# A recurrent mixer in chunks of 64 tokens, with each chunk as an affine map of the state

## What is computed

```python
def wkv7_scan(r, w, k, v, a, b):
    """S_t = S_{t-1} diag(w_t) + (S_{t-1} a_t) b_t^T + v_t k_t^T ; y_t = S_t r_t.
    All inputs (B, S, H, N) f32; state (B, H, N_v, N_k)."""
    def step(state, inp):
        r_t, w_t, k_t, v_t, a_t, b_t = inp
        sa = jnp.einsum('bhvk,bhk->bhv', state, a_t)
        state = (state * w_t[:, :, None, :] + sa[..., None] * b_t[:, :, None, :]
                 + v_t[..., None] * k_t[:, :, None, :])
        return state, jnp.einsum('bhvk,bhk->bhv', state, r_t)
    s0 = jnp.zeros((B, H, N, N), jnp.float32)
    _, ys = lax.scan(step, s0, xs)
    return jnp.moveaxis(ys, 0, 1)
```

## Time and profile before

| | us |
|---|---|
| median of 3 runs | 3302.31 (3301.39 to 3302.34) |
| the profiled execution | 3304.38 |
| its span, first to last instruction | 3302.4 |
| TensorE, matmul | 3173.8 (96%) |
| VectorE | 1703.5 (52%) |
| ScalarE | 1066.7 (32%) |
| GpSimd | 1972.7 (60%) |

### The profile page before, as it was taken

The page is one execution under the profiler, slowest core; times in us unless marked ns, Lnnn a source line. Parts: engine busy times, 40 slices in busy tenths (PEclk is TensorE's granted clock), DMA queues, the critical chain, the costliest instruction groups (busy, mean ns, idle before and its releaser), DMA issues.

```text
span 3302.4 us, 54354 instructions
## 1 busy us (share of the span) xinstructions
PE 3173.8 (96%) x19314; PEld 2521.1 (76%) x19314; DVE 1703.5 (52%) x2741; ACT 1066.7 (32%) x1988; POOL 1972.7 (60%) x2607
## 2 busy tenths in 40 slices
PE   6998999999999999899999999999999999999999
PEld 4766777777888888577778888887667777888887
DVE  4456777765554335542645554446551635565345
ACT  2153434432221113542635321113552535331112
POOL 4624333336588885246465888886327373898886
PEclk8999999999999999999999999999999999999999
DMA  5341111112233232112121322232102121223322
GB/s 210 138 163 51 46 40 40 40 34 77 93 98 100 95 96 65 32 52 83 40 82 58 96 96 96 95 96 83 45 27 95 46 83 46 93 93 100 98 95 96
DMA packets 70794, 265.22 MB, mean 80 GB/s; under 512 B 7744, under 2 KB 7872, under 8 KB 67520
## 3 DMA queue, kind: packets, MB, share of 16 engines
q1 hardware_dynamic: 68288, 257.59, 23.7%
q10 hardware_dynamic: 2304, 4.83, 0.4%
HBM read 260.29 MB, written 2.10 MB: 79 GB/s over the span
## 4 chain that ended last, share of the span: by engine, by line
PE 83%; DVE 9%; ACT 5%; issue 1%; DMA 1%; SPq 0%; DVEq 0%; ACTq 0%
PE psum_a L579 10%; PE psum_a L583 10%; PE psum_a L582 10%; PE psum_d L579 7%; PE psum_d L583 6%; PE psum_d L582 6%; PE psum_d L645 5%; PE psum_a L737 3%; PE psum_d L840 2%; PE psum_a L767 2%; PE psum_a L771 2%; PE psum_a L770 2%; PE psum_a L608 1%; PE psum_a L611 1%; PE psum_a L612 1%
## 5 line engine op out<-in xcount | busy, mean ns | idle before, releaser
L3383 POOL TENSOR_TENSOR w_lo<-raw,w_hi 128x256 fp32r<-128x256 f32 x1736 | 1425.7, 852 | 36.3
L3377 POOL TENSOR_TENSOR mark<-mark 128x1 f32<-128x1 f32 x432 | 105.2, 244 | 1248.0 <-PE psum_a L579 627.7
L579 PE MATMUL psum_a<-h_hi,w_hi 128*128 128x512 f32 x1600 | 631.9, 395 | 0.0
L583 PE MATMUL psum_a<-h_hi,w_lo 128*128 128x512 f32 x1600 | 623.7, 390 | 0.0
L582 PE MATMUL psum_a<-h_lo,w_hi 128*128 128x512 f32 x1600 | 623.3, 390 | 0.0
L3378 POOL TENSOR_SCALAR w_hi<-raw 128x1024 fp32r<-128x1024 f32 x434 | 459.6, 1059 | 33.3 <-DMA raw<-in_weights 33.3
L579 PEld LDWEIGHTS psum_a<-h_hi,w_hi 128*128 128x128 f32 x1600 | 300.8, 188 | 71.7 <-issue 10.7
L582 PEld LDWEIGHTS psum_a<-h_lo,w_hi 128*128 128x128 f32 x1600 | 300.9, 188 | 63.2 <-issue 2.2
L583 PEld LDWEIGHTS psum_a<-h_hi,w_lo 128*128 128x128 f32 x1600 | 300.7, 188 | 63.2
L579 PE MATMUL psum_d<-split,w_hi 128*128 128x512 f32 x848 | 329.9, 389 | 0.0
L582 PE MATMUL psum_d<-split,w_hi 128*128 128x512 f32 x848 | 329.9, 389 | 0.0
(11 more groups left out here) (407 smaller groups left out, 5524.7 us busy)
## 6 DMA issues: line engine op xcount, KB each, us to landing
raw<-in_weights SPq DMA_DIRECT2D x434, 512.0 KB, 3.4
plain<-in_ada SPq DMA_DIRECT2D x20, 1024.0 KB, 6.9
arena<-in_ada SPq DMA_DIRECT2D x4, 1024.0 KB, 16.9
x<-in_x SPq DMA_DIRECT2D x1, 2048.0 KB, 12.2
x<-in_x ACTq DMA_DIRECT2D x1, 2048.0 KB, 9.9
out<-x SPq DMA_DIRECT2D x8, 256.0 KB, 3.5
arena<-in_pe ACTq DMA_DIRECT2D x2, 512.0 KB, 3.6
const<-in_const ACTq DMA_DIRECT2D x1, 906.0 KB, 8.5
```

Source lines behind the costliest of these rows:

```text
L579: m = pe.eng.matmul(dst, wh, hi(t), start=t == 0, stop=False)
L583: m = pe.eng.matmul(dst, wl, hi(t), start=False, stop=t == k - 1)
L3377: eng.tensor_tensor(b.mark[:, 1:2], b.mark[:, 0:1], b.mark[:, 0:1], ALU.add)
L3383: m = eng.tensor_tensor(lo[:, part], b.raw[:, s, part], hi[:, part].bitcast(F32), ALU.subtract)
```

## The change

The chunks become 64 tokens long (eight instead of four), and a chunk is brought into the form of an affine map of the state, so that the chain is one product for each chunk:

- In the levels the four chunks with their `first`, `second`, `third` go. In their place stand six `step` products (two 64x64 products each, with one VectorE operation on 64 columns each), two at each of k=1 to 3, and one batch of outputs at k=4 (`outputs`, fourteen products, added by `dve_rwkv_outputs`).
- The maps themselves are made for all chunks at once: `inputs` between `g2` and gate of the next round, `maps` between gate and branch, with `act_rwkv_inputs`, `act_rwkv_outputs` on ScalarE and `dve_rwkv_transitions` (six operations) on VectorE.
- The start of the inverse takes 64x64 products on both sides (`pe_units`), as the inverse needs no block beyond 64. The two corners, the diagonal and the four map chunks go; two sets of `pe_units`, the turned AR (`pe_own_rows`), four transposes and the values product come.
- One scan over 512 columns, with zeros at the chunk starts in a tile `R_ONES`, replaces four scans and two column operations; two exponentials over 512 columns replace eight over 128 and two small ones. Three memsets set this up ahead of round 0.
- In the tail the order becomes gate, `inputs`, gate, `maps`, two gates in quarters with the six steps between the quarters, `outputs`, half a gate, mean, half a gate, variance. The gates of the tail now go through ring "a".

The diff, cut to the added lines of what is spoken of here:

```diff
+def pe_units(pe, ring, *terms, width=HD):
+    tiles = [pe.tile(ring) for _ in range(2)]
+    pe.eng.wait_ge(tiles[1].free, pe.emptied(tiles[1]))
+    for v in range(4):
+        for k, (lhsT, rhs) in enumerate(terms):
+            for n, (row, out) in enumerate(((0, 0), (1, 1), (0, 1), (1, 0))):
+                m = pe.eng.matmul(tiles[row].ps[ROWS[out], v * width:(v + 1) * width], lhsT(v, row, out), rhs(v, row, out),
+                                  start=k == 0, stop=k == len(terms) - 1)
+                if k == len(terms) - 1 and v == 3 and n >= 2:
+                    m.then_inc(tiles[row].full, pe.up("full_" + ring))
+    return tiles[1]
...
+def pe_own_rows(pe, ring, lhsT, rhs, chunks):
+    tl = pe.tile(ring)
...
+    for c in chunks:
+        for r in ROWS:
+            m = pe.eng.matmul(tl.ps[r, c * HD:(c + 1) * HD], lhsT(r, c), rhs(r, c), start=True, stop=True)
+    m.then_inc(tl.full, pe.up("full_" + ring))
+    return tl
...
         pe, b = self.pe, self.b
...
+        pe, b = self.pe, self.b
+        G, H = block(b.R_GH[:, :, 0]), block(b.R_GH[:, :, 1])
+        pe.eng.wait_ge(self.solved.free, pe.taken(self.solved))
+        pe_units(pe, "d", (G, lambda v, row, out: b.R_BL[ROWS[row], 2 * v + out]), width=P)
+        self.state = pe_units(pe, "d", (block(b.R_BL[:, :, 0]), H), (block(b.R_KN), block(b.R_VN)))
+        self.local = pe_units(pe, "a", (H, block(b.R_BL[:, :, 1])), (block(b.R_VN), block(b.R_KA[:, :, 1])))
+    def states(self, c):
...
+        return self.b.R_EQ[:, 0] if c == 1 else self.b.R_S[:, c]
+    def step(self, c):
+        pe, b = self.pe, self.b
+        pe.eng.wait_ge(self.state.free, pe.taken(self.state))
+        tl = self.state = pe.tile("d")
...
+        for r in ROWS:
+            m = pe.eng.matmul(tl.ps[r, 0:HD], b.R_PR[r, c, 0], self.states(c)[r], start=True, stop=True)
+        m.then_inc(tl.full, pe.up("full_d"))
+    def outputs(self):
         pe, b = self.pe, self.b
...
+    A, R, B, K = block(AR[:, :, 0]), block(AR[:, :, 1]), block(chunks(b.R_BH)), block(chunks(b.R_KH))
     more = j + 1 < KD
     pe_features(pe, "a", "g2", of(b.s_hi, b.s_lo, 1), 1)
+    if chain:
+        chain.inputs()
     pe_features(pe, "a", "gate", H)
+    if chain:
+        chain.maps()
     pe_features(pe, "d", "branch", of(b.s_hi, b.s_lo, 2), 2)
     pe.eng.wait_ge(pe.sem["rk_ready"], pe.due("rk_ready"))
     pe_plain(pe, "d", b.pair, b.R_T)
...
         else:
             pe.eng.wait_ge(normal.free, pe.taken(normal))
...
+        z = pe_units(pe, "d", (block(b.R_LT), block(b.R_TN)))
         inverse = pe_turned(pe, [b.R_TN[:, 2 * v:2 * v + 2].rearrange("p u t -> p (u t)") for v in range(4)])
...
+        if chain and k <= 3:
+            chain.step(2 * k - 1)
+        if chain and k == 4:
+            chain.outputs()
         if k == 2 and more:
             pe_rwkv_receptance(pe)
         if k == 4 and more:
             pe_rwkv_value(pe)
         if k in (2, 4) and not more:
             pe_features(pe, "a", "gate", H)
...
+        if chain and k == 5:
+            pe_rwkv_mean(pe)
         pe.eng.wait_ge(inverse.free, pe.taken(inverse))
         pe.eng.wait_ge(z.free, pe.taken(z))
...
+        normal = pe_units(pe, "d", (block(b.R_TW), block(b.R_Z)))
+        if chain and k <= 3:
+            chain.step(2 * k)
         if k == 3 and more:
             pe_rwkv_length(pe)
...
+    for src in (b.R_V, b.R_BH, b.R_KH):
+        turned = pe_turned(pe, [src[:, q * P:(q + 1) * P] for q in range(NQ)])
+    pe_units(pe, "d", (B, R))
+    maps = pe_units(pe, "d", (K, lambda v, row, out: AR[ROWS[row], 2 * v + out]), width=P)
+    pe_own_rows(pe, "a", lambda r, c: AR[r, c, 0], lambda r, c: b.ident[r, r], range(8))
     pe.eng.wait_ge(normal.free, pe.taken(normal))
...
+    inverse = pe_turned(pe, [b.R_TN[:, 2 * v:2 * v + 2].rearrange("p u t -> p (u t)") for v in range(4)])
+    pe.eng.wait_ge(turned.free, pe.taken(turned))
+    pe.eng.wait_ge(maps.free, pe.taken(maps))
+    values = pe_units(pe, "a", (block(b.R_KA[:, :, 0]), block(b.R_VN)))
...
+    pe_features(pe, "a", "gate", H)
+    chain.inputs()
+    pe_features(pe, "a", "gate", H)
+    chain.maps()
+    for first in (1, 4):
+        tl = pe.tile("a")
...
+        for n in range(4):
+            m = pe_product(pe, tl.ps, "gate", *H, KD, None, part=range(2 * n, 2 * n + 2))
+            if n < 3:
+                chain.step(first + n)
+        m.then_inc(tl.full, pe.up("full_a"))
+    chain.outputs()
+    tl = pe.tile("a")
...
+    pe_product(pe, tl.ps, "gate", *H, KD, None, part=range(0, 4))
     pe_rwkv_mean(pe)
...
+    a.eng.wait_ge(a.sem[a.last], a.own())
+    a.eng.activation(b.R_PB[:, :, 1:], chunks(b.R_CUM), ACT.Exp, scale=-DECAY).then_inc(a.sem["act_step"], a.up("act_step"))
+    a.eng.wait_ge(a.sem[a.last], a.own())
+    a.eng.activation(b.R_CUM, b.R_CUM, ACT.Exp, scale=DECAY).then_inc(a.sem["decays"], a.up("decays"))
...
+        v.eng.tensor_tensor_scan(b.R_CUM, b.R_ONES, b.R_SW, 0.0, ALU.mult, ALU.add)\
...
     if step == 2:
...
+def dve_rwkv_maps(v):
+    b = v.b
+    both = v.each(b.const[:, C_MASK4 + 2 * P:C_MASK4 + 3 * P], 4)
+    inclusive = v.each(b.const[:, C_MASK4 + 2 * P + HD:C_MASK4 + 3 * P], 4)
+    for row in range(2):
...
+        v.eng.tensor_tensor(other_rows(b.R_BL[:, :, 1], row), v.units(HD), inclusive, ALU.mult)\
...
+    for row in range(2):
...
+        v.eng.tensor_tensor(other_rows(b.R_KA.rearrange("p u m t -> p u (m t)"), row), v.units(P), both, ALU.mult)\
...
+def dve_rwkv_transitions(v, j):
+    b, AR, eye = v.b, v.b.R_AR[j % 2], v.each(v.b.const[:, C_EYE:C_EYE + HD], 4)
+    for row in range(2):
...
+        ps = v.units(P)
...
+        v.eng.tensor_tensor(other_rows(b.R_PR[:, :, 0], row), ps[:, :, 0:HD], eye, ALU.add)\
...
+        v.eng.tensor_tensor(other_rows(b.R_PR[:, :, 1], row), ps[:, :, HD:], other_rows(AR[:, :, 1], row), ALU.add)\
...
+    ends = b.R_E[j % 2].rearrange("p (v o) -> p v o", o=2)
+    for row in range(2):
...
+        v.eng.tensor_tensor(other_rows(b.R_EQ, row), v.units(HD), ends[:, :, row].unsqueeze(2).to_broadcast([P, 4, HD]), ALU.mult)\
...
 def dve_rwkv_state(v, j, c):
     b = v.b
...
+    v.eng.scalar_tensor_tensor(b.R_S[:, c + 1], v.bank()[:, 0:HD], b.R_E[j % 2][:, c:c + 1], b.R_EQ[:, c], ALU.mult, ALU.add)\
...
+def dve_rwkv_outputs(v):
+    b = v.b
...
+    v.eng.tensor_tensor(b.R_Y[:, HD:], v.bank()[:, HD:], b.R_Y[:, HD:], ALU.add).then_inc(v.sem["free_d"], v.up("free_d"))
 def dve_rwkv(v, j):
...
+    b = v.b
     more = j + 1 < KD
     dve_rwkv_prepare(v, j)
+    if j:
+        dve_rwkv_transitions(v, j - 1)
...
+            v.eng.tensor_tensor(other_rows(b.R_Z, row), v.units(HD), level, ALU.mult).then_inc(v.sem["free_d"], v.up("free_d"))
+        if j and k <= 3:
+            dve_rwkv_state(v, j - 1, 2 * k - 1)
+        if j and k == 4:
+            dve_rwkv_outputs(v)
         if k == 1:
             dve_rwkv_receptance(v, j)
...
+            v.eng.tensor_tensor(dst, dst, v.units(HD), ALU.add).then_inc(v.sem["free_d"], v.up("free_d"))
+        if j and k <= 3:
+            dve_rwkv_state(v, j - 1, 2 * k)
         if k in (1, 3) and more:
...
+    dve_rwkv_mixed(v, KD - 2)
+    dve_rwkv_transitions(v, KD - 1)
+    for c in range(1, 7):
         dve_rwkv_state(v, KD - 1, c)
...
+        dve_rwkv_low(v, c - 1)
+    dve_rwkv_outputs(v)
     dve_rwkv_centered(v)
     dve_rwkv_low(v, KD - 2)
     dve_rwkv_normed(v, KD - 1)
```

396 lines of the change are left out of this document (112 added, 284 removed).

## The result

The changed kernel takes 3312.66 us, median of 20 runs (3302.24 to 3320.79); the kernel before takes 3303.82 in 20 runs beside them (3300.3 to 3309.75). The ratio is 1.0024, 95% interval 1.0017 to 1.0032: slower by 8.8 us, inside the range of 3286 to 3318, but not the "no change" of the forecast. The profiled execution is one of the longer ones: 3317.57 us, span 3315.8, 4.9 us above the median.

The account below looks back on a forecast made before the run. VectorE's string was taken to set the level starts, TensorE to bound only part of the stage. Before round 0 -4.5, round 0 -2.2, rounds 1-6 +13.8, round 7 -0.6, tail -6.0: +0.5 us, forecast 3302.8, range 3286 to 3318.

Parts of the forecast that it names:

- The clean sum: Round 2 at full clock, all stretches added: +4.7 + 0 - 1.6 - 2.2 + 0.9 - 1.9 = -0.1 us, no gain.
- its clock terms for the rounds: Rounds 1 to 6, per round: +2.5 us half clock behind k=5, -0.5 already paid today, +0.4 for falls between k=1 and k=2.
- head: Start of a round, g2 to the first set of k=1: `inputs` and `maps` products lie on TensorE's path, loss 4.7 us.
- The reading that round 0 shows what the levels take without a chain: Levels of round 0 before the change: VectorE sets level starts, so a whole chain costs only 4 us a round.
- the length wait: Ahead of round 0, TensorE's wait before the first length product: falls from 4.01 us to about 1.
- its signs of being wrong: Wait under 2 us or full clock at k=5, head under 20 us, or rounds more than 2 from 63 us.
- I allow 0.4 a round for falls between k=1 and k=2: Rounds 1 to 6, early levels: an allowance of 0.4 us a round for TensorE's clock falling there.
- The falls behind k=5: From k=5 to the next round: half clock behind the longer wait, 2.3 to 3 us a round, taken 2.5.
- the slower rival: The clock also falls between k=1 and k=2, 1.7 us each; 3316 us with a dearer 128-column set; chance 0.24.
- Said -2.2: Round 0: only the new ending and start count, -2.2 us.
- -4.5 ahead of round 0: Ahead of round 0: wide exponentials 2.0, one scan 1, clock 1.5 us saved; -4.5 us (-5.5 to -2).
- changes of tiling: Into and out of 64-row work on TensorE: four more changes a round, 0.3 us together (0 to 0.6).

Follow-up runs that it names:

- the two filled kernels: Changed kernel and kernel before, each with unused idle-time products put into TensorE's waits ahead of k=2 and k=5 (before: k=2 in round 0 only): 3285.28 and 3300.17 us.
- the filled kernel: Changed kernel with unused TensorE products, four ahead of the wait before k=2 and six ahead of the wait before k=5: 3285.28 us.
- the last experiment: The version with three moves, with the wide scan and two wide exponentials taken apart into four scans and eight exponentials of 128 columns: 3264.67 us.
- the version with three moves: Changed kernel with VectorE's receptance behind the sums of k=1, reciprocal's string behind the last masks, two finishing operations from k=2 to k=4: 3263.09 us.

## Why the prediction was wrong by this much

**What held.** The clean sum. Without its clock terms for the rounds (6 x 2.4 = 14.4) it was 0.5 - 14.4 = -13.9 us; the two filled kernels are 14.9 apart. That the whole agrees so well is in part luck. By parts their profiled executions, counted from the first key product, differ by -5.5 up to g2 (said -4.5), +1.5 in round 0 (-2.2), -0.8 in rounds 1 to 6 (-0.6) and -8.8 in round 7 with the tail (-6.6): the miss in round 0 is made up by the two ends. For a round at full clock it said -0.1; six rounds of the filled kernels differ by 0.8, or 0.14 a round. By stretch, against the table: head +4.1 for +4.7, k=1 to 2 +0.05 for 0, 2 to 3 -1.4 for -1.6, 3 to 4 -2.3 for -2.2, 4 to 5 +1.0 for +0.9, ending -1.9 for -1.9. The reading that round 0 shows what the levels take without a chain carried all of it. The tail gave 6.2 for 6.0. Most of the signs that it named came: waits at k=5 of 2.93 to 3.81 us in rounds 0 to 6, released by the sums; half clock behind six of these seven; rounds of 63.9 us on the mean for 63; the length wait at 0.19 us for "about 1"; the tail at 37.6 for 38 to 39. But two of its signs of being wrong came as well, in single rounds: full clock behind k=5 in round 4, and rounds 1, 3 and 4 at 66.07, 65.45 and 59.22 us, more than 2 from 63. They belong to the step that follows.

**Where it fell: the clock behind k=2.** The step is "I allow 0.4 a round for falls between k=1 and k=2". In the profiled execution k=2 to k=3 took 11.23, 11.50, 11.08, 8.89, 11.84 and 10.40 us in rounds 1 to 6, 11.5 us more in sum than the filled kernel's 53.5, where the sum had 2.4. The falls behind k=5 cost 11.0 in the six rounds, where it had 15, which hid part of the miss at k=2; what before lost in its rounds was 3.4 for 3. So the six rounds lost 19 net by the clock where I had 14.4, and round 7, for which I had none, lost 2.8 more in the same place (11.72 against 8.92). This was the slower rival, with its place and its mechanism; its price was low (1.7 said for a fall, 2.3 measured on the mean of the five in rounds 1 to 6). The clock fell there in seven of the eight rounds, all but round 4. I gave it 0.24 since round 0 before had kept its clock through 1.79 us. The same round shows how little that was worth. The set at k=2 waited 1.79 us again, and here are the windows behind it, before and after:

```profile
280.60:284.00 3.40, 3.40 (x46) 2.92 (x47) 2.89 (x8) 2.00 (x3) 0.00 (x0) 1.00 0.00 0
```
```profile
278.50:281.90 3.40, 3.40 (x41) 2.89 (x34) 3.05 (x5) 1.50 (x2) 0.00 (x0) 0.50 0.02 5
```

The same wait, and 1.00 in the one, 0.50 in the other. What came before was not the same: the changed kernel had half clock from 264.9 to 268.3 us, behind a wait that before does not have (next paragraph). Of the versions with nothing put in at k=2 of round 0, all five with such a fall in the head fell at k=2 again, behind 1.05 to 1.80 us, and of the five without it one did (1.05 us). No experiment separates the two.

**Round 0.** Said -2.2, came +3.2. Two steps were missing. The squares were 4 us earlier, as the sum said, but VectorE's reciprocal and products behind them were not, so the bonus product got a wait that before did not have:

```profile
263.46 1.12 PE L646 MATMUL psum_d<-arena,const 128*128 128x512 f32 x2 [2.27 <-DVE arena L2479]
```

Of the 5.9 us won ahead of g2 this gives 2.3 back, and the last experiment shows that the wide operations are worth 1.4 us at that product. The rest is half clock behind this wait and at k=2: eight versions have this wait of some 2.26 us with nothing put into it, and the clock fell behind it in seven. "-4.5 ahead of round 0" was a right number for the wrong point: the path there ends at the bonus product, not at g2.

**Prices.** The maps' sets were dearer on paper than on the chip: from 380.84 to the next product 1.04 us (1.05 taken), and from 387.56 to the branch product 2.90 for 3.55, since a set with two terms takes 1.05 us, not 1.25. For changes of tiling I took 0.3 a round; behind the 64-row sets of the head the first 128-row product (381.88, 390.46) takes 0.50 us with 0.33 to the next start, where 0.23 is usual, so 0.1 each. The Trainium skill, TensorEngine Tiling (Array Packing), Key Properties, says that such a change drains the array; these rows are compatible with that, at a price of 0.1 us, and do not separate a drain from another cost of the change.

**What stays open.** The changed kernel's profiled execution is 2.3 us longer behind the stage, in code that is the same; there the profiled executions of the studied kernels lie between 2519 and 2529 us whatever was changed, with their own falls of the clock, so I count it as no part of the change. Which single wait brings a fall is not settled: 2.93 us ahead of k=5 in round 4 did not, 0.95 in one round of the version with three moves did. What the fourteen profiled executions give is a count. Of TensorE's waits of 0.8 us or more between 240 and 790 us that began at full clock, half clock set in during the wait or within 3 us behind it in 8 of 200 below 1.1 us, 3 of 21 from 1.1 to 1.5, 6 of 13 from 1.5 to 2.0, and 64 of 72 above 2.0.

## What to carry to other kernels

Work that leaves a chain of small steps does not leave the path if another engine's string sets the next start; it turns into a wait, and on TensorE the wait then costs again, in the clock of the dense products behind it. So count a wait of 2 us or more that stands ahead of matmul-bound work as 1.4 to 2.9 us more, in each place by itself, and look whether what the releasing engine does ahead of the release is needed by then: here three moves of VectorE's operations turned a loss of 8.8 us into a gain of 41.9. A move that gains in one version can lose in the other; the place to which an operation goes must have slack in that kernel.
